# One MLP operand of two parts, squares on another engine and another split of the softmax, in a kernel of four transformer layers

## The chip, the cores and the metric
One NeuronCore of a Trainium2 chip runs the whole program. The time is what the device takes for one execution, in microseconds (us); the kernel's number is the median of several executions.

## What is computed
Two blocks of two layers each, for one sequence of 256 tokens with 1024 features, all in 32-bit floating point. Every layer adds a mixer and, in the first block, an MLP to the residual x:

```python
def sq_relu_mlp(h, w_in, w_out):          # 1024 -> 4096 -> 1024
    a = jax.nn.relu(h @ w_in)
    return (a * a) @ w_out
...
p = jax.nn.softmax(logits, axis=-1)       # in MLA, MoBA and FoX, 8 heads each
...
def l2_norm(x):                           # of GDN's q and k, per head and token
    return x * lax.rsqrt(jnp.sum(x * x, axis=-1, keepdims=True) + EPS)
```

The order is MLA attention, MLP 0, MoBA attention, MLP 1 (first block), then GDN (a gated delta rule, with a causal convolution ahead and triangular inverses by head and chunk) and FoX (attention with forget gates; second block).

## The kernel before
All weights, 140 MB, are streamed from HBM once, as 136 chunks of at most 128 x 2048 numbers (1 MB). MLA has chunks 0 to 13, MLP 0 has 14 to 45, MoBA 46 to 61, MLP 1 62 to 93, GDN 94 to 114, FoX 115 to 135. Each passes through the same five steps, each on one engine, in rings of three buffers:

- SyncE loads the chunk into `raw` (`load(c)`), once `lo(c-3)` has read that buffer.
- ScalarE rounds it to the format TensorE multiplies at full rate, fp32r: `whi` (`hi(c)`), once TensorE has finished chunk c-3.
- VectorE (POOL for six chunks of GDN) makes the rest, `wlo = raw - whi` (`lo(c)`).
- TensorE multiplies. The activations too are split, into `xh` and `xl`. A product is three matmuls into the same PSUM region: whi·xh, whi·xl, wlo·xh.

Every engine's program is one written-out list of steps, so what is queued on an engine is served in that order. TensorE's list counts chunks in quarters: `to(18, 2)` means "run chunk quarters up to quarter 2 of chunk 18", and the small steps (`score`, `turn_p`, `sums`, `bias_mm`, ...) stand between. `half(c)` and `full(c)` are the semaphore values after the second and fourth quarter of chunk c.

An MLP goes by 8 groups g of 512 hidden features. The order of its chunks is: up 0 (two chunks), up 1, down 0, up 2, down 1, and so on to down 7. In an up-projection chunk (kind `pw`) quarter m is the 128 hidden features of one weight column tile, k runs over four tiles of the 1024 inputs, and the tokens (256 columns) are what moves; two m share one PSUM bank, and groups alternate between banks 4, 5 and 6, 7. Then, by half group `hf` (512 numbers per partition): ScalarE's `relu_square` takes Relu out of PSUM and squares it; VectorE's `hidden` rounds that to `oth` and puts the rest into `otl`, which are the stationary operands of the down-projection (kind `back`, 512 columns moving).

In a softmax, `logits` (VectorE) adds mask or bias, takes the maximum and negates it; `exp` (ScalarE) also gives the sum; `divide` (VectorE) inverts the sum and multiplies the two parts of 128 and 256 columns; `turn_p` (TensorE) transposes. In GDN, `k_square` (VectorE) and `q_square` (POOL) square one head of 256 columns each, into four buffers `sqp`, and TensorE's `sums(h)` adds over the features with 8 or 16 matmuls of one column. Banks 4 to 7 of PSUM also serve all small steps in turn (`ring`), and `take` makes TensorE wait until the bank's last reader is done.

```python
mm(o, wh[:, k, s], h_[:, kk, :], kk == 0 and m % 2 == 0)
mm(o, wh[:, k, s], l_[:, kk, :], False)
tok = mm(o, wl[:, k, s], h_[:, kk, :], False)
```

These are an up-projection's three matmuls. In the profile all matmuls have line 480, all transposes 488, ScalarE's work 1354, VectorE's products and sums of two tensors 2208, those with a scalar 2211 and 2214.

Of the kernel before, what the change touches and what calls it, by code (L numbers as in the profile page):

```python
# [130 lines left out]
def bass_two_blocks(nc, A, out):  # L131

    ctx = ExitStack()
    with ctx:
# [19 lines left out]
        xh = sb("xh", [128, 8, T], F32R)  # L154
        xl = sb("xl", [128, 8, T], F32R)
# [44 lines left out]
        def rsq_tiles(n, own=6):  # L200
# [25 lines left out]
        s_sc, s_sx, s_mx, s_ex, s_dv, s_tn, s_pt, s_vl, s_oh, s_ol = (sem(n) for n in (  # L226
            "s_sc", "s_sx", "s_mx", "s_ex", "s_dv", "s_tn", "s_pt", "s_vl", "s_oh", "s_ol"))

        s_rel, s_sqr, s_hid = sem("s_rel"), sem("s_sqr"), sem("s_hid")
# [5 lines left out]
        (s_gx, s_ga, s_gg, s_beta, s_cm, s_cum, s_pre, s_acc, s_cv, s_sl, s_k2, s_q2, s_st, s_sst, s_lnr, s_rw, s_rwt, s_rT,  # L235
         s_rb, s_dt, s_ed, s_sel, s_kq, s_ba, s_sv, s_vt, s_v, s_zs) = (sem("g_" + n) for n in (
             "gx", "ga", "gg", "beta", "cm", "cum", "pre", "acc", "cv", "sl", "k2", "q2", "st", "sst", "lnr", "rw", "rwt", "rT",
# [223 lines left out]
        def tensor_program(eng):  # L461
# [35 lines left out]
            def quarter(c, q):  # L497
# [87 lines left out]
                elif kind == "pw":  # L585
                    half_, m = q // 2, q
                    b = d["pair"] + half_
                    if d["hk"] == 0 and q % 2 == 0:
                        if stage == "gdn":
                            take(b, s_pre, 2 * d["g"] + half_ + 1)  # L590
                        elif stage == "fox":
                            take(b, s_fz, 2 * d["g"] + half_ + 1)
                        else:
                            take(b, s_rel, 16 * int(stage[3]) + 2 * d["g"] + half_ + 1)
# [195 lines left out]
            def sums(h):  # L790
                L.wait_ge(s_k2, h + 1)
                L.wait_ge(s_q2, h + 1)
# [41 lines left out]
            def inv_ops(g):  # L834
                ops = (oth, otl) if g < 2 else (xh.rearrange("p k n -> p (k n)"), xl.rearrange("p k n -> p (k n)"))
                return [x[:, 1024 * (g % 2) + 512 * i:1024 * (g % 2) + 512 * i + 512] for x in ops for i in range(2)]
# [126 lines left out]
            to(1, 3)  # L963
# [16 lines left out]
            qp_T(0)  # L980
            score_pair(0)
            q_T(1)
            to(8, 2)
            qp_T(1)
            to(9, 2)
            turn_p("mla", 0)
            score_pair(1)
            turn_p("mla", 1)
# [6 lines left out]
            qp_T(2)  # L995
            q_T(2)
            to(11, 0)
            q_T(3)
            turn_p("mla", 2)
            turn_p("mla", 3)  # L1000
            score_pair(2)
# [3 lines left out]
            score_pair(3)  # L1005
            turn_p("mla", 4)
            to(11, 3)
            turn_p("mla", 5)
            turn_p("mla", 6)
            value("mla", 4)  # L1010
            turn_p("mla", 7)
            value("mla", 5)
            value("mla", 6)
            to(12, 0)
# [8 lines left out]
            to(22, 0)  # L1023
# [5 lines left out]
            to(30, 0)  # L1029
# [22 lines left out]
            to(52, 3)  # L1052
            turn_p("moba", 0)
            turn_p("moba", 1)
            to(53, 0)
            turn_p("moba", 2)
            to(53, 2)
# [10 lines left out]
            value("moba", 2)  # L1068
            score("moba", 4)
            score("moba", 5)  # L1070
            value("moba", 3)
            to(57, 3)
            turn_p("moba", 4)
            score("moba", 6)
# [40 lines left out]
            to(105, 3)  # L1115
# [15 lines left out]
            inv_0(0)  # L1131
            row_bc(5)
            to(109, 1)
            kq(4)
# [3 lines left out]
            inv_0(1)  # L1138
            row_bc(7)
            to(109, 3)  # L1140
            kq(6)
            kq(7)
            to(110, 0)
            inv_w(1, 1)
            v_T(0, 0)
            v_T(0, 1)
            inv_x(1, 1)
            inv_w(0, 1)
            v_T(1, 0)
            inv_x(0, 1)  # L1150
            inv_v(1, 1)
            inv_w(1, 2)
            v_T(1, 1)
# [44 lines left out]
            inv_x(3, 1)  # L1198
            inv_v(2, 1)
            sol(1, 0)  # L1200
# [3 lines left out]
            sol(3, 0)  # L1204
            inv_x(3, 2)
            sol(2, 0)
# [6 lines left out]
            sol(1, 1)  # L1213
            sol(0, 1)
            sol(3, 1)
# [3 lines left out]
            inv_w(3, 4)  # L1219
            sol(1, 3)  # L1220
            sol(0, 2)
# [28 lines left out]
            inv_y(3)  # L1250
            sol(4, 0)
            sol(5, 0)
            out_T(1)
            sol(6, 0)
            sol(4, 1)
            sol(5, 1)
            sol(7, 0)
            sol(6, 1)
            sol(4, 2)
            sol(5, 2)  # L1260
            sol(7, 1)
            sol(6, 2)
            sol(4, 3)
            sol(5, 3)
            sol(7, 2)
            sol(6, 3)
            sol(7, 3)
# [15 lines left out]
            to(117, 2)  # L1283
            across(1)
            to(120, 1)
            few_T(1)
            to(121, 2)
            c_mm()
            to(121, 3)
            c_T()  # L1290
            to(122, 0)
            c_bc(0)
            c_bc(1)
            c_bc(2)
            c_bc(3)
            to(126, 0)
            qk_T("fox", "k0", 0)
            qk_T("fox", "k0", 1)
            to(126, 1)
            qk_T("fox", "q0", 0)  # L1300
            qk_T("fox", "q0", 1)
            to(126, 2)
            score("fox", 0)
            score("fox", 1)
            c_bc(4)
            to(126, 3)
            score("fox", 2)
            score("fox", 3)
            c_bc(5)
            to(127, 1)  # L1310
            turn_p("fox", 0)
            to(128, 2)
            turn_p("fox", 1)
            to(128, 3)
            turn_p("fox", 2)
            to(130, 0)
            value("fox", 0)
            value("fox", 1)
            turn_p("fox", 3)
            to(130, 1)  # L1320
            qk_T("fox", "q1", 0)
            to(130, 2)
            qk_T("fox", "q1", 1)
            c_bc(6)
            c_bc(7)
            to(131, 0)
            qk_T("fox", "k1", 0)
# [4 lines left out]
            score("fox", 6)  # L1332
            score("fox", 7)
            to(132, 0)
            value("fox", 2)
            value("fox", 3)
            turn_p("fox", 4)
            to(132, 1)
            turn_p("fox", 5)
            to(133, 0)  # L1340
# [4 lines left out]
            to(133, 1)  # L1345
# [5 lines left out]
        def scalar_program(eng):  # L1351
# [68 lines left out]
            def exp(stage, j):  # L1420
# [8 lines left out]
                act(Q[:, 128:384], S[:, 128:384], ACT.Exp, bias=ng[:, 1:2], accum_out=su[:, 1:2]).then_inc(s_ex, 1)  # L1429

# [118 lines left out]
            def relu_square(i, g, hf):  # L1549
                v = g % 2  # L1550
                e = 16 * i + 2 * g + hf + 1
                c = C0[f"mlp{i}"] + (1 if g == 0 else 4 * g - 1)
                rel = view(2048 * v + 512 * hf, 512)
                sqr = view(2048 * v + 1024 + 512 * hf, 512)
                L.wait_ge(s_w, half(c) if hf == 0 else full(c))
                if g >= 2:
                    L.wait_ge(s_hid, e - 4)
# [20 lines left out]
            def conv_silu(i):  # L1578
                nm, g, hf = CONV[i // 2][0], int(CONV[i // 2][1]), i % 2
                L.wait_ge(s_cv, i + 1)  # L1580
                act((kS if nm == "k" else qS)[:, 4 * g + 2 * hf:4 * g + 2 * hf + 2, :], acc2[i % 4], ACT.Silu).then_inc(s_sl, 1)

# [32 lines left out]
            def inv_ops(g):  # L1615
                ops = (oth, otl) if g < 2 else (xh.rearrange("p k n -> p (k n)"), xl.rearrange("p k n -> p (k n)"))
                return [x[:, 1024 * (g % 2) + 512 * i:1024 * (g % 2) + 512 * i + 512] for x in ops for i in range(2)]
# [71 lines left out]
            hi(1)  # L1689
            hi(2)  # L1690
            squares("mla")
# [4 lines left out]
            rsq("mla_x")  # L1696
            proj_scale()
            hi(5)
            hi(6)
# [3 lines left out]
            c_hi(2)  # L1703
            rsq("mla_c")
            c_hi(3)
            c_hi(4)
            kv_copy(0, 0)
# [6 lines left out]
            rsq("mla_k0")  # L1714
            uq_copy(1, 0)
            uq_copy(1, 1)
            rsq("mla_q0")
# [3 lines left out]
            k_copy(0, 0)  # L1721
            rsq("mla_q1")
            k_copy(0, 1)
            q_copy(0)
            qp_copy(0)
            hi(10)
            kv_copy(1, 0)
            kv_copy(1, 1)
            k_squares(1)
            exp("mla", 0)  # L1730
            uq_copy(2, 0)
            rsq("mla_k1")
            q_copy(1)
            qp_copy(1)
            exp("mla", 1)
            uq_copy(2, 1)
            uq_copy(3, 0)
            q_squares(2)
            p_copy("mla", 0)
            p_copy("mla", 1)  # L1740
            o_hi("mla", 0)
            o_hi("mla", 1)
            rsq("mla_q2")
# [3 lines left out]
            hi(11)  # L1747
            exp("mla", 3)
            rsq("mla_q3")
            qp_copy(2)  # L1750
            k_copy(1, 0)
            k_copy(1, 1)
            q_copy(2)
            q_copy(3)
            p_copy("mla", 2)
            p_copy("mla", 3)
            hi(12)
            qp_copy(3)
            exp("mla", 4)
            o_hi("mla", 2)  # L1760
            o_hi("mla", 3)
            hi(13)
            exp("mla", 5)
            exp("mla", 6)
            exp("mla", 7)
            p_copy("mla", 4)
            p_copy("mla", 5)
            p_copy("mla", 6)
            o_hi("mla", 4)
            o_hi("mla", 5)  # L1770
            o_hi("mla", 6)
            p_copy("mla", 7)
            hi(14)
            o_hi("mla", 7)
# [5 lines left out]
            hi(16)  # L1780
            hi(17)
            hi(18)
            hi(19)
            relu_square(0, 0, 0)
            relu_square(0, 0, 1)
            relu_square(0, 1, 0)
            hi(20)
            hi(21)
            hi(22)
            hi(23)  # L1790
            relu_square(0, 1, 1)
            relu_square(0, 2, 0)
            relu_square(0, 2, 1)
            hi(24)
            hi(25)
            hi(26)
# [1999 lines left out]
```

## Time and profile before

| | us |
|---|---|
| three runs | 933.17, 934.24, 937.74 |
| median | 934.24 |
| the profiled execution, whole | 937.91 |
| its span, first to last instruction | 936.2 |

| engine | busy us | share | instructions |
|---|---|---|---|
| TensorE (PE) | 906.1 | 97% | 5944 |
| VectorE (DVE) | 625.1 | 67% | 1035 |
| ScalarE (ACT) | 512.0 | 55% | 766 |
| GpSimd (POOL) | 110.4 | 12% | 144 |

A row of a group has the count behind an x, the busy time and the mean of one instruction, then the engine's idle time ahead of such instructions and what ended it. A row of the timeline begins with start and duration in us, and names in brackets the idle time before it and its releaser. Matmuls overlap in it, so the distance of two starts says more than a duration.

### The profile page before, as it was taken

Reading aid. Unit: us, or ns where it says so; the run is one execution under the profiler, and the core shown is the slowest. Engines: PE = TensorE matmul, PEld = TensorE weight load, DVE = VectorE, ACT = ScalarE, POOL = GpSimd, SP = SyncE. Lnnn points to the kernel's source line nnn. Section 1 sums busy time; section 2 is a strip of 40 time slices with the busy share of each in tenths; the row PEclk is TensorE's granted clock in tenths of the full one; section 3 lists DMA queues with packets and bytes.
Section 4 is the critical chain, followed back from the end, with each engine's and each line's share of the span. In section 5 each row is a group of like instructions: output and inputs, shape, how many; then the busy total and the mean of one; then the engine's idle time right before and its main releaser. Section 6 shows DMA issues by size and latency. Waiting matters only on the chain.

```text
span 936.2 us, 14470 instructions
## 1 busy us (share of the span) xinstructions
PE 906.1 (97%) x5944; PEld 815.6 (87%) x5944; DVE 625.1 (67%) x1035; ACT 512.0 (55%) x766; POOL 110.4 (12%) x144
## 2 busy tenths in 40 slices
PE   5898999999999999999999999999999999999997
PEld 5776899999998888899999998999998987798886
DVE  5798766566455686655454445898886776856884
ACT  5787454345354667544454453664446664747662
POOL 0055000000000000000000000007476612000000
PEclk9999999999999999999999999999899999999999
DMA  7442356275554633455645544562511302345431
GB/s 245 146 139 87 134 182 245 90 263 178 176 192 137 224 123 141 156 183 176 211 154 207 186 174 138 182 224 90 170 56 68 136 1 90 127 164 207 134 113 46
DMA packets 61681, 142.74 MB, mean 152 GB/s; under 512 B 5296, under 2 KB 7344, under 8 KB 61616
## 3 DMA queue, kind: packets, MB, share of 16 engines
q1 hardware_dynamic: 61616, 141.82, 44.4%
q8 instruction: 47, 0.77, 0.3%
q14 instruction: 18, 0.15, 0.0%
HBM read 140.76 MB, written 1.05 MB: 151 GB/s over the span
## 4 chain that ended last, share of the span: by engine, by line
PE 84%; POOL 4%; issue 4%; DVE 4%; ACT 2%; SPq 1%; DMA 0%; POOLq 0%; DVEq 0%; ACTq 0%
PE ps L480 81%; PE ps L488 4%; POOL arena L3379 3%; DVE wlo L2208 1%; POOL wlo L3379 1%; SPq L3513 1%; POOL arena L3429 1%; ACT arena L1354 1%; ACT whi L1354 0%; DVE arena L2208 0%; DMA pint<-rel_bias_table_dram 0%; DVE oth L2208 0%; DVE X L2208 0%; ACT otl L1354 0%; DVE arena L2211 0%
## 5 line engine op out<-in xcount | busy, mean ns | idle before, releaser
L2208 DVE TENSOR_TENSOR wlo<-raw,whi 128x2048 fp32r<-128x2048 f32 (+3 forms) x130 | 287.4, 2218 | 162.1 <-ACT whi L1354 162.0
L1354 ACT ACTIVATE whi<-raw 128x2048 fp32r<-128x2048 f32 (+3 forms) x136 | 251.1, 1853 | 264.1 <-PE ps L480 225.5
L480 PE MATMUL ps<-xh,whi 128*128 128x256 f32 (+2 forms) x784 | 224.3, 286 | 0.3 <-DVE wlo L2208 0.3
L480 PE MATMUL ps<-xl,whi 128*128 128x256 f32 (+2 forms) x784 | 222.7, 284 | 0.0
L480 PE MATMUL ps<-xh,wlo 128*128 128x256 f32 (+2 forms) x784 | 222.7, 284 | 0.0
L480 PE MATMUL ps<-whi,oth 128*128 128x512 f32 x384 | 151.7, 395 | 0.0
L480 PEld LDWEIGHTS ps<-xh,whi 128*128 128x128 f32 (+2 forms) x784 | 149.9, 191 | 1.6 <-DVE wlo L2208 0.4
L480 PEld LDWEIGHTS ps<-xl,whi 128*128 128x128 f32 (+2 forms) x784 | 149.9, 191 | 1.0
L480 PEld LDWEIGHTS ps<-xh,wlo 128*128 128x128 f32 (+2 forms) x784 | 149.8, 191 | 0.4
L480 PE MATMUL ps<-whi,otl 128*128 128x512 f32 x384 | 149.7, 390 | 0.0
L480 PE MATMUL ps<-wlo,oth 128*128 128x512 f32 x384 | 149.7, 390 | 0.0
L480 PE MATMUL ps<-whi,xh 128*128 128x512 f32 (+2 forms) x264 | 104.1, 394 | 1.9 <-DVE wlo L2208 0.7
L480 PE MATMUL ps<-whi,xl 128*128 128x512 f32 (+2 forms) x264 | 100.3, 380 | 0.0
L480 PE MATMUL ps<-wlo,xh 128*128 128x512 f32 (+2 forms) x264 | 100.2, 380 | 0.0
L3379 POOL TENSOR_TENSOR arena<-arena 128x64 f32<-128x64 f32 (+1 forms) x56 | 28.2, 529 | 544.3 <-ACT arena L1354 539.4
L480 PEld LDWEIGHTS ps<-whi,otl 128*128 128x128 f32 x384 | 72.1, 188 | 15.3
L480 PEld LDWEIGHTS ps<-whi,oth 128*128 128x128 f32 x384 | 72.2, 188 | 14.1 <-issue 0.2
L480 PEld LDWEIGHTS ps<-wlo,oth 128*128 128x128 f32 x384 | 72.2, 188 | 13.9
L1354 ACT ACTIVATE arena<-ps 128x512 f32<-128x512 f32 (+3 forms) x104 | 49.5, 492 | 38.2 <-PE ps L480 28.1
L480 PE MATMUL ps<-arena 128*128 128x128 f32 (+3 forms) x384 | 63.4, 319 | 0.6 <-issue 0.5
L1354 ACT ACTIVATE arena<-arena 128x512 f32<-128x512 f32 (+5 forms) x94 | 58.4, 641 | 10.2 <-DVE arena L2211 6.0
L480 PEld LDWEIGHTS ps<-whi,xh 128*128 128x128 f32 x264 | 50.3, 191 | 11.0 <-DVE wlo L2208 2.4
(147 smaller groups left out, 1108.2 us busy)
## 6 DMA issues: line engine op xcount, KB each, us to landing
raw<-mlp_w_in_dram SPq DMA_DIRECT2D x32, 1024.0 KB, 5.2
raw<-mlp_w_out_dram SPq DMA_DIRECT2D x32, 1024.0 KB, 4.9
raw<-gdn_w_in_dram SPq DMA_DIRECT2D x16, 1024.0 KB, 5.3
raw<-moba_w_qkv_dram SPq DMA_DIRECT2D x12, 1024.0 KB, 5.1
raw<-kv_w_dram SPq DMA_DIRECT2D x8, 1024.0 KB, 5.3
raw<-fox_w_in_dram SPq DMA_DIRECT2D x8, 1024.0 KB, 5.4
raw<-mla_w_o_dram SPq DMA_DIRECT2D x4, 1024.0 KB, 5.1
raw<-moba_w_o_dram SPq DMA_DIRECT2D x4, 1024.0 KB, 6.1
```

The lines of the kernel that those rows point to most:

```text
L480: return eng.matmul(o, l, r, start=start, stop=True, skip_group_check=True)
L488: return eng.transpose(o, i, ident)
L1354: return eng.activation(o, i, f, **kw)
L2208: return eng.tensor_tensor(o, a, b, f)
L3379: return eng.tensor_tensor(o, a, b, f)
L3429: ins = eng.affine_select(out=x, in_=x, pattern=[[1, 128]], compare_op=ALU.is_ge, fill=0.0, base=-strict, channel_multiplier=-1)
L3513: eng.dma_start(o, i).then_inc(s_in, 16)
```

## The change
- **MLPs.** `xh` and `xl` become the two halves of one tensor `xhl`, [128, 8, 2, 256]. In the up-projection the first two matmuls become one with 512 moving columns, over both halves; wlo·xh stays, with 256. Each m now fills a bank (4 + m), columns 0 to 255 and 256 to 511 being the two terms. ScalarE's `half_copy` copies the right halves to SBUF, VectorE's `hidden_sum` adds the left ones and forms max(a, 0)·a, ScalarE's `hidden_hi` rounds that to `oth`, and VectorE's `hidden` only makes `otl`. The banks are free again after the adds. All groups use the same four banks.
- **GDN.** One Square on ScalarE per head (`qk_square`, q and k together, 512 columns) takes the place of `k_square` and `q_square`.
- **Softmaxes.** The maxima are written out negated by the reduction; `over_sum` (VectorE) inverts the sum, `divide` (ScalarE) multiplies by it as a scaled copy.
- **Orders.** All engines' lists are rearranged: many small steps stand some quarters earlier or later, neighbouring loads are swapped, and `levels_in` (448 KB for GDN's masks), which waits until MLA's down-projection is done, moves from behind `load(22)` to between `load(17)` and `load(16)`.

```diff
-        xh = sb("xh", [128, 8, T], F32R)
-        xl = sb("xl", [128, 8, T], F32R)
+        xhl = sb("xhl", [128, 8, 2, T], F32R)
+        xh, xl = xhl[:, :, 0, :], xhl[:, :, 1, :]
+        xpair = xhl[:, :, :, :].rearrange("p k z n -> p k (z n)")
...
-                    b = d["pair"] + half_
+                    mlp_ = stage[:3] == "mlp"
+                    b = 4 + m if mlp_ else d["pair"] + half_
+                    if d["hk"] == 0 and mlp_:
+                        take(b, s_sqr, 2 * (16 * int(stage[3]) + 2 * d["g"] + half_) + 1)
...
+                        if mlp_:
+                            mm(P[b][:, :], wh[:, k, s], xpair[:, kk, :], kk == 0)
+                            tok = mm(P[b][:, 0:256], wl[:, k, s], xh[:, kk, :], False)
+                            continue
...
             def sums(h):
                 L.wait_ge(s_k2, h + 1)
-                L.wait_ge(s_q2, h + 1)
...
-            to(103, 0)
+            to(105, 1)
             sums(0)
-            to(103, 2)
             sums(1)
-            to(104, 0)
+            to(105, 2)
             sums(2)
             sums(3)
-            to(105, 0)
+            to(105, 3)
             sums(4)
             sums(5)
-            to(105, 1)
             cum_mm()
             sums(6)
             sums(7)
-            to(105, 3)
+            to(106, 1)
             rw_T()
...
-                act(rel, P[4 + 2 * v + hf][:, :], ACT.Relu).then_inc(s_rel, 1)
-                L.wait_ge(s_rel, e)
-                act(sqr, rel, ACT.Square).then_inc(s_sqr, 1)
+                for j in range(2):
+                    ins = act(rel[:, 256 * j:256 * j + 256], P[4 + 2 * hf + j][:, 256:512], ACT.Copy)
+                ins.then_inc(s_rel, 1)
+
+            def hidden_hi(i, g, hf):
...
+                act(oth[:, o:o + 512], sqr, ACT.Copy).then_inc(s_hh, 1)
...
+            def divide(stage, j):
...
+                L.wait_ge(s_rcp, a.base + j + 1)
+                act(Q[:, 0:128], Q[:, 0:128], ACT.Copy, scale=rc[:, 0:1])
+                act(Q[:, 128:384], Q[:, 128:384], ACT.Copy, scale=rc[:, 1:2]).then_inc(s_dv, 1)
...
+            def qk_square(h):
...
+                act(view(18944 + 512 * (h % 2), 512, "p (a n) -> p a n", a=2),
+                    view(0, 4096, "p (a h n) -> p a h n", a=2, h=8)[:, :, h, :], ACT.Square).then_inc(s_k2, 1)
...
-                eng.reduce_max(mx[:, 0:1], S[:, 0:128], AX)
-                L.step(eng.reduce_max(mx[:, 1:2], S[:, 128:384], AX))
-                L.settle()
-                ts(ng, mx, -1.0, None, ALU.mult).then_inc(s_mx, 1)
+                eng.reduce_max(ng[:, 0:1], S[:, 0:128], AX, negate=True)
+                eng.reduce_max(ng[:, 1:2], S[:, 128:384], AX, negate=True).then_inc(s_mx, 1)
...
+            def hidden_sum(i, g, hf):
...
+                L.wait_ge(s_rel, e)
+                if g >= 2:
+                    L.wait_ge(s_hid, e - 4)
+                for j in range(2):
+                    s = rel[:, 256 * j:256 * j + 256]
+                    ins = tt(s, P[4 + 2 * hf + j][:, 0:256], s, ALU.add)
+                ins.then_inc(s_sqr, 1)
+                L.wait_ge(s_sqr, 2 * e - 1)
+                stt(sqr, rel, 0.0, rel, ALU.max, ALU.mult).then_inc(s_sqr, 1)
```

## Rows read from the trace of the kernel before

**Rows 1.** The page's busy times: us, share of the span, instructions.
```profile
PE 906.1 (97%) x5944; PEld 815.6 (87%) x5944; DVE 625.1 (67%) x1035; ACT 512.0 (55%) x766; POOL 110.4 (12%) x144
```
**Rows 2.** Busy us (x instructions) by stretch, then granted clock, DMA share, GB/s.
```profile
60.00:100.00 40.00, 36.71 (x222) 30.09 (x221) 34.02 (x91) 31.44 (x79) 15.79 (x38) 1.00 0.32 108
408.00:585.00 177.00, 177.00 (x1144) 162.24 (x1143) 92.66 (x74) 81.20 (x72) 0.00 (x0) 1.00 0.52 179
640.00:663.00 23.00, 22.86 (x181) 22.80 (x182) 21.35 (x48) 11.34 (x14) 15.30 (x12) 0.92 0.45 155
661.00:663.00 2.00, 2.00 (x11) 2.00 (x11) 1.69 (x11) 1.03 (x3) 0.00 (x0) 0.50 1.05 410
700.00:780.00 80.00, 76.78 (x596) 71.40 (x595) 54.80 (x105) 52.73 (x101) 38.28 (x38) 1.00 0.17 60
```
**Rows 3.** The chain that ended last, its piece in MLP 1: start, us, what.
```profile
408.18 176.79 PE ps L480 x1140
```
**Rows 4.** TensorE's timeline in MLP 1, where the kind of chunk changes.
```profile
431.19 0.40 PE L480 MATMUL ps<-whi,oth 128*128 128x512 f32 x1
...
442.09 0.28 PE L480 MATMUL ps<-xh,whi 128*128 128x256 f32 x1
...
453.61 0.40 PE L480 MATMUL ps<-whi,oth 128*128 128x512 f32 x1
```
**Rows 5.** VectorE's groups by shape, 112 to 300 us (MLP 0).
```profile
L2208 DVE TENSOR_TENSOR otl<-arena,oth 128x512 fp32r<-128x512 f32 x16 | 11.1, 692 | 0.5
...
L2217 DVE CAST oth<-arena 128x512 fp32r<-128x512 f32 x16 | 6.8, 422 | 3.5 <-ACT arena L1354 3.5
...
L2208 DVE TENSOR_TENSOR arena<-ps,cst 128x256 f32<-128x256 f32 x4 | 1.7, 420 | 1.0 <-PE ps L480 1.0
```
**Rows 6.** ScalarE's groups by shape, 112 to 300 us: Square, then Relu.
```profile
L1354 ACT ACTIVATE arena<-arena 128x512 f32<-128x512 f32 x16 | 10.1, 634 | 0.5
L1354 ACT ACTIVATE arena<-ps 128x512 f32<-128x512 f32 x16 | 9.3, 582 | 1.8 <-PE ps L480 1.8
```
**Rows 7.** Timeline in MLP 1: VectorE's difference for chunk 84, TensorE's first matmul of it.
```profile
523.11 2.29 DVE L2208 TENSOR_TENSOR wlo<-raw,whi 128x2048 fp32r<-128x2048 f32 x1 [2.41 <-ACT whi L1354]
...
531.80 0.28 PE L480 MATMUL ps<-xh,whi 128*128 128x256 f32 x1
```
**Rows 8.** Timeline at MLP 0's start: the cast of chunk 16.
```profile
117.94 1.92 ACT L1354 ACTIVATE whi<-raw 128x2048 fp32r<-128x2048 f32 x1 [2.49 <-DMA raw<-mlp_w_in_dram]
```
**Rows 9.** Groups by shape, 60 to 100 us: VectorE's divisions, ScalarE's exponentials.
```profile
L2211 DVE TENSOR_SCALAR arena<-arena,st 128x256 f32<-128x256 f32 x8 | 2.9, 357 | 0.0
L2211 DVE TENSOR_SCALAR arena<-arena,st 128x128 f32<-128x128 f32 x8 | 2.5, 307 | 0.3
...
L1354 ACT ACTIVATE arena<-arena,st 128x256 f32<-128x256 f32 x8 | 4.0, 500 | 0.0
...
L1354 ACT ACTIVATE arena<-arena,st 128x128 f32<-128x128 f32 x8 | 3.2, 397 | 1.1 <-DVE st L2211 1.1
```
**Rows 10.** Timeline in MLA: POOL's rotary work of the last query pair, TensorE's transpose.
```profile
80.22 1.12 POOL L3379 TENSOR_TENSOR arena<-arena,st 128x256 f32<-128x256 f32 x1 [0.71 <-DVE st L2214]
...
87.39 0.44 PE L488 MATMUL ps<-cst,arena 128*128 128x128 f32 x2 [2.32 <-POOL arena L3379]
```
**Rows 11.** Groups by shape, 630 to 663 us: squares and first taps on VectorE and POOL.
```profile
L2208 DVE TENSOR_TENSOR arena<-arena 128x256 f32<-128x256 f32 x7 | 7.1, 1023 | 0.1
...
L3379 POOL TENSOR_TENSOR arena<-arena 128x256 f32<-128x256 f32 x6 | 7.6, 1275 | 3.7 <-PE ps L480 3.7
```
**Rows 12.** TensorE's timeline in GDN: the last clump of small matmuls and after.
```profile
654.22 1.84 PE L480 MATMUL ps<-cst,arena 128*128 128x1 f32 x16
...
657.44 0.73 PE L480 MATMUL ps<-st,cst 128*128 128x8 f32 x6
658.31 2.43 PE L480 MATMUL ps<-cst,arena 128*128 128x1 f32 x16
...
661.17 0.41 PE L480 MATMUL ps<-xh,wlo 128*128 128x256 f32 x1
661.38 0.41 PE L480 MATMUL ps<-xh,whi 128*128 128x256 f32 x1
```

More of the change, by code:

```diff
@@ L1689, in scalar_program @@
             hi(1)
+            squares("mla")
             hi(2)
-            squares("mla")
             hi(3)
@@ L1797, in scalar_program @@
             hi(27)
+            half_copy(0, 3, 0)
+            half_copy(0, 3, 1)
+            hidden_hi(0, 3, 0)
+            squares("mlp0")
             hi(28)
-            relu_square(0, 3, 0)
-            relu_square(0, 3, 1)
             hi(29)
@@ L1931, in scalar_program @@
             hi(84)
-            relu_square(1, 5, 0)
-            relu_square(1, 5, 1)
+            half_copy(1, 5, 0)
+            half_copy(1, 5, 1)
+            hidden_hi(1, 5, 0)
             hi(85)
@@ L2907, in vector_program @@
             lo(15)
+            bias_ind(3)
             lo(16)
+            hidden_sum(0, 0, 0)
+            hidden_sum(0, 0, 1)
             lo(17)
             lo(18)
-            bias_ind(3)
             hidden(0, 0, 0)
+            hidden_sum(0, 1, 0)
+            lo(19)
+            bias_ind(4)
             hidden(0, 0, 1)
-            lo(19)
+            hidden(0, 1, 0)
+            bias_add(3)
+            hidden_sum(0, 1, 1)
+            bias_ind(5)
             lo(20)
-            bias_add(3)
@@ L2931, in vector_program @@
             bias_ind(6)
             bias_ind(7)
-            lo(26)
+            hidden(0, 2, 1)
+            hidden_sum(0, 3, 0)
             bias_add(6)
+            hidden(0, 3, 0)
             lo(27)
+            lo(28)
+            bias_add(7)
             bias_ind(8)
-            bias_ind(9)
-            bias_add(7)
-            hidden(0, 3, 0)
-            lo(28)
+            hidden_sum(0, 3, 1)
             lo(29)
             lo(30)
+            bias_ind(9)
             lo(31)
+            hidden_sum(0, 4, 0)
@@ L2957, in vector_program @@
+            lo(35)
+            lo(36)
+            bias_add(10)
+            bias_add(11)
+            hidden_sum(0, 5, 1)
+            lo(37)
+            lo(38)
             hidden(0, 5, 0)
-            bias_add(10)
-            lo(36)
-            lo(37)
-            bias_add(11)
+            lo(39)
             hidden(0, 5, 1)
-            lo(38)
-            lo(39)
+            hidden_sum(0, 6, 0)
+            hidden_sum(0, 6, 1)
             lo(40)
@@ L2967, in vector_program @@
             lo(42)
+            hidden(0, 6, 0)
+            variance(0)
             lo(43)
-            hidden(0, 6, 0)
+            hidden_sum(0, 7, 0)
+            hidden_sum(0, 7, 1)
             hidden(0, 6, 1)
@@ L3044, in vector_program @@
             lo(65)
+            hidden_sum(1, 0, 0)
+            hidden_sum(1, 0, 1)
             lo(66)
+            lo(67)
             hidden(1, 0, 0)
             hidden(1, 0, 1)
-            lo(67)
-            hidden(1, 1, 0)
-            hidden(1, 1, 1)
+            hidden_sum(1, 1, 0)
+            hidden_sum(1, 1, 1)
             lo(68)
             lo(69)
+            hidden(1, 1, 0)
             lo(70)
+            hidden(1, 1, 1)
+            hidden_sum(1, 2, 0)
+            hidden_sum(1, 2, 1)
             lo(71)
@@ L3056, in vector_program @@
             lo(73)
-            lo(74)
-            lo(75)
             hidden(1, 2, 0)
             hidden(1, 2, 1)
-            hidden(1, 3, 0)
+            lo(74)
+            hidden_sum(1, 3, 0)
+            hidden_sum(1, 3, 1)
+            lo(75)
             lo(76)
@@ L3577, in sync_program @@
             load(10)
-            load(12)
             load(11)
             load(13)
+            load(12)
+            load(15)
             load(14)
-            load(15)
             load(17)
+            levels_in()
             load(16)
@@ L3631, in sync_program @@
             load(63)
+            load(65)
             load(64)
-            load(65)
             load(66)
@@ L3662, in sync_program @@
             load(93)
+            load(96)
             load(95)
-            load(96)
             load(97)
```

757 lines of the change are left out of this document (404 added, 353 removed).

## The prediction

> **What bounds the kernel now.** I read the busy shares first: TensorE 906.1 us, 97% of the span, VectorE 67%, ScalarE 55% [rows 1]. A mean over stages says little, so next the busy time by stage: in the MLPs TensorE has no hole at all (177.00 of 177.00 us in the second), between 60 and 100 us (MLA) it is busy 36.7 of 40 and between 700 and 780 us (GDN's triangular inverses) 76.8 of 80 [rows 2]. The chain that ended last says the same by what released what: in the second MLP 176.79 us of it are unbroken TensorE [rows 3]. So in an MLP a change is worth what it takes from TensorE's own stream; outside, what it takes from a wait that TensorE really has.
>
> A busy TensorE can still be fed better or worse, and durations mislead here: one matmul lasts 0.28 or 0.39 us but they overlap. What counts is the distance between starts. From 431.19 to 442.09 us stand 48 matmuls of 512 columns: 10.90/48 = 0.2271 us each. From 442.09 to 453.61 us stand 96 of 256 columns: 11.52/96 = 0.1200 us [rows 4]. The difference, 0.1071 us for 256 columns, is the rate of the 2.4 GHz level (the granted clock is 1.00 there [rows 2]); what is left, 0.013 us, is paid once per matmul whatever its width.
>
> **MLP up-projection.** Before, a weight tile costs three 256-column matmuls (hi·xh, hi·xl, lo·xh); after, one of 512 (hi·[xh|xl]) and one of 256 (lo·xh). The columns are the same 768, one matmul is gone: 3 x 0.1200 = 0.3600 becomes 0.2271 + 0.1200 = 0.3471, 0.0129 us less. The weight of 1024 x 4096 has 8 x 32 = 256 tiles of 128 x 128, both MLPs 512: **−6.6 us**, all on the path. Bounds: zero if the mixed sequence doesn't keep the pitch of the pure ones; on the other side the 768 columns alone, 3 x 0.1071 = 0.3213 us a tile, −19.8 us, which no row comes near. I take 6.6, since both pitches are read in the very stage.
>
> The Trainium skill (TensorE: Matmul & The Clock Gate, "Back-to-back issue gap") speaks against it: by it a matmul costs its columns and some 2.5 ns. By that rule 512 fewer save 1.3 us. The rows show 13 ns.
>
> The two halves must now be added. Per half group (32 in both MLPs) ScalarE's Relu and Square of 512 (0.58 + 0.64 us) become two copies of 256 out of PSUM and one cast of 512; VectorE's cast and difference (0.42 + 0.69 us) become two adds of 256 (0.42 each by its 256-wide work), a max-times of 512 and the difference (0.69 each): about 2.2 instead of 1.1 us [rows 5, 6]. A group of 22 us then asks VectorE for four weight differences of 2.29 and 4.4 = 13.6 us, ScalarE for about 10. That lies beside TensorE and costs nothing as long as the weight differences come early: the one ending at 525.40 us is of the chunk that TensorE begins at 531.80 (one chunk stands between), 6.4 us ahead [rows 7]. This cover is the thing to lose: VectorE serves in order, and what is queued behind a `hidden_sum` that waits for ScalarE's copy is the next `lo`, on which both TensorE and, through the ring of three, SyncE's next load wait.
>
> Banks: a group now fills four banks instead of two, so the next group waits for its adds. Only groups 0 and 1 of each MLP are adjacent; elsewhere 10.9 us of down-projection lie between. There the first half has two quarters (2 x 4 tiles x 0.347 = 2.8 us) for two copies and two adds (about 1.7 us): nothing, but with 1 us to spare. In the first MLP this meets a moved step on SyncE: `levels_in`, which waits for the end of MLA's down-projection, now stands ahead of `load(16)`. Its 448 KB take 2.6 us at the stage's 179 GB/s, and the cast of chunk 16 already waited 2.49 us for its DMA and began at 117.94 us [rows 2, 8]. Copy and add of group 0 stand behind that cast and its difference. I put +0.5 us on it (0 to +3). The other swaps of loads next to each other I cost at nothing: with three ring slots both are asked for within a chunk's time.
>
> **Softmaxes (24 heads).** VectorE loses a small negation and two multiplications (0.31 + 0.36), ScalarE gains two scaled copies: by its exponentials of the same shapes 0.40 and 0.50 us, less the 0.1 us by which neighbours overlap, 0.8 us a head. Only the busy share says whether it matters: MLA from 60 to 100 us has VectorE at 34.0 and ScalarE at 31.4 of 40 [rows 2, 9]. Moving 8 x 0.8 us shifts which is fuller but frees the side that feeds the rotary terms: TensorE's one long hole, 2.32 us before 87.39, ends with POOL's rotary work, and POOL had itself waited for VectorE, until 80.22 us [rows 10]. With `over_sum` short and `rsq_b` of the queries ahead, POOL starts about 1 us sooner. I take −1.2 us for MLA (−3 to +2.5, the latter if ScalarE, the fuller engine then, is late with the copies that TensorE's transposes wait for). In MoBA and FoX TensorE is covered by projections: 0 (−1 to +1).
>
> **GDN.** 16 products of 256 columns leave VectorE and POOL (7.1 us for 7 and 7.6 for 6 in 630 to 663 us, so over 1 us each, while the two engines run side by side) and become 8 of 512 on ScalarE, 0.64 us each as its Squares in the MLP: 5.1 us, in a stretch where it is busy 11.3 of 23 [rows 2, 6, 11]. None of this is on the chain: TensorE is busy 22.86 of 23 us there. It changes when `sums` can stand: they move from quarters (103,0)…(105,1) to (105,1)…(105,3), the last four close together on two alternating buffers, each pair waiting for ScalarE behind the one before: +0.3 to +1 us, against −1 for VectorE and POOL being free ahead of the decays. Net −0.5 (−3 to +3). The inverses themselves aren't touched.
>
> **The clock.** The profiled execution lost time at 659 us: behind 16 and, 1.4 us on, 6 + 16 matmuls of 1 or 8 columns the granted clock fell to 0.50, the 1.2 GHz level, and 256 columns went at 0.213 us instead of 0.120 [rows 2, 12]. The two quarters behind it are 24 of these, 2.2 us more, and some small ones before; I put 2.8 us on it. After the change 22 such small matmuls stand in one clump, with two of 8 ahead, so I expect the same odds of a fall. The profiled run took 937.91 us, the timed ones 933.17, 934.24 and 937.74: a median that does without the fall fits (937.9 − 2.8 = 935.1).
>
> **The sum.** −6.6 + 0.5 − 1.2 − 0.5 = −7.8. On the profiled execution's 937.9 us this is 930.1; on the median of the runs, 3.7 below that execution, it is 926.4.
>
> **Rivals.**
> (A) *The per-matmul cost isn't there to save.* The 0.013 us could come with the change of weights and width rather than with each matmul, and the mixed sequence keep 0.360 us a tile. Then the MLPs give nothing and 934.2 + 0.5 − 1.2 − 0.5 = 933.0 is left. For it: only pure sequences can be read. Against: every matmul of the pure ones changes its weights too. 6%. The page of the Trainium skill named above points this way; by its 2.5 ns the time would be 1.3 us lower, 931.7, as an estimate.
> (B) *The drain holds the weights back: slower than before.* Place: VectorE's queue in the MLPs, `lo` behind `hidden_sum` and `hidden`, these behind ScalarE's `half_copy`. From half(c) the chain runs 0.8 + 0.8 + 0.7, again for the second half 2.8 us later, then 0.6 + 0.7, then `lo` 2.3: about 8.8 us, against 8.3 until TensorE needs the chunk after next. If the order lets a whole drain stand ahead of `lo`, and handing over costs a little more than I count, 1 us is lost in each of 16 groups: 926.4 + 16 = 942. It decides from the point where VectorE's lead of 6.4 us is used up; most groups have a `lo` between the halves, which speaks against. 6%.
> (C) *Given back outside*: ScalarE late in MLA, the clump of `sums` waits, the entry to the first MLP costs 2 to 3 us: −6.6 + 2.5 + 1 + 1 = −2.1, so 932. 10%.
> (D) *More than forecast*: MLA's hole closes and GDN gains 3: 934.2 − 6.6 − 2.5 − 3 = 922. 8%.
> The forecast itself, 926.4 with 923 to 929.5: 70%.
>
> **Numbers.** Faster by over 0.5% (below 929.6; 0.5% is about what a measurement of this kernel can tell): the forecast, D, and a little of C: 0.80. Same (929.6 to 938.9): most of C, A: 0.14. Slower: 0.06. The range 921 to 932 takes in D, the bounds of MLA, GDN and the clock, and C; it leaves out B.
>
> **What would show it.** Starts 0.227 and 0.120 us apart by turns in the MLPs, pairs of up-projection chunks 11.10 instead of 11.52 us long; TensorE without a hole in them; each MLP 3.3 us shorter; ScalarE's squares of 512 near 650 us. It would be wrong if the 512-column matmul or its follower took longer, or if the weight differences ended less than 1 us ahead of their chunk.

## The result, and the profile after

| | before | after |
|---|---|---|
| median of 7 runs each, us | 937.11 (933.17 to 937.74) | 931.19 (929.36 to 931.48) |
| the profiled execution, us | 937.91 | 929.36 |
| its span, us | 936.2 | 927.6 |

The ratio is 0.9943 (0.9928 to 0.9959): 0.57% faster, −5.9 us, where the forecast was −7.8 us from a base of 934.24. The time of 931.19 us lies in the range given (921 to 932), 4.8 us above the predicted 926.4.

Busy times on the page of after (us, share of the span, instructions), against [rows 1]: TensorE has 512 instructions less and is busy 6.4 us less, VectorE 5.2 us and ScalarE 19.8 us more, GpSimd 11.0 us less.

```profile
PE 899.7 (97%) x5432; PEld 785.9 (85%) x5432; DVE 630.3 (68%) x1019; ACT 531.8 (57%) x854; POOL 99.4 (11%) x136
```

The same stretches by the windows view of after (columns as in [rows 2], the MLP window starting at its own 404):

```profile
60.00:100.00 40.00, 37.05 (x216) 30.71 (x215) 29.33 (x66) 32.82 (x90) 13.93 (x33) 1.00 0.33 118
...
404.00:581.00 177.00, 177.00 (x898) 149.88 (x897) 108.79 (x107) 82.14 (x91) 0.00 (x0) 1.00 0.52 179
```

In MLP 1 TensorE still has no hole (177.00 of 177.00), though VectorE went from 92.66 to 108.79 us. The chain of waits of after has both MLPs as one unbroken piece of TensorE (start, us, what):

```profile
111.40 181.17 PE ps L483 x1100
...
403.67 175.26 PE ps L483 x884
```

The second answers to [rows 3]: 176.79 became 175.26, that is −1.5 us with 256 matmuls less, where −3.3 was forecast. TensorE's timeline of after shows why. First the places where the kind of chunk changes, as in [rows 4], then a stretch inside an up-projection:

```profile
437.20 0.39 PE L483 MATMUL ps<-xhl,whi 128*128 128x512 f32 x1
...
448.49 0.40 PE L483 MATMUL ps<-whi,oth 128*128 128x512 f32 x1
...
459.44 0.39 PE L483 MATMUL ps<-xhl,whi 128*128 128x512 f32 x1
```
```profile
440.01 0.40 PE L483 MATMUL ps<-xhl,whi 128*128 128x512 f32 x1
440.25 0.28 PE L483 MATMUL ps<-xhl,wlo 128*128 128x256 f32 x1
440.37 0.40 PE L483 MATMUL ps<-xhl,whi 128*128 128x512 f32 x1
440.61 0.28 PE L483 MATMUL ps<-xhl,wlo 128*128 128x256 f32 x1
440.72 0.40 PE L483 MATMUL ps<-xhl,whi 128*128 128x512 f32 x1
```

Two up-projection chunks (32 weight tiles) took 448.49 − 437.20 = 11.29 us, so 0.3528 us a tile: neither the 0.3600 of before nor the forecast 0.3471. A 512-column matmul is followed after 0.23 to 0.24 us, a 256-column one after 0.11 to 0.12. The down-projection behind it took 10.95 us against 10.90 before [rows 4]. One cycle of up and down is 22.24 us against 22.42: 0.18 us saved, 16 times is 2.9 us. The two pieces of the chain together, 182.69 + 176.79 before and 181.17 + 175.26 after, give 3.0.

The cover held. VectorE's and ScalarE's groups by shape, 112 to 300 us in after, against [rows 5, 6]:

```profile
L2300 DVE TENSOR_TENSOR arena<-ps,arena 128x256 f32<-128x256 f32 x32 | 12.0, 418 | 11.9 <-ACT arena L1360 11.9
L2306 DVE SCALAR_TENSOR_TENSOR arena<-arena 128x512 f32<-128x512 f32 x16 | 11.1, 693 | 0.5
...
L2300 DVE TENSOR_TENSOR otl<-arena,oth 128x512 fp32r<-128x512 f32 x16 | 10.6, 685 | 0.1
```
```profile
L1360 ACT ACTIVATE arena<-ps 128x256 f32<-128x256 f32 x32 | 10.5, 381 | 23.4 <-PE ps L483 23.4
L1360 ACT ACTIVATE oth<-arena 128x512 fp32r<-128x512 f32 x16 | 9.9, 627 | 4.8 <-DVE arena L2306 4.8
```

Two adds of 0.418, 0.693 and 0.685 make 2.2 us a half group, as forecast.

### The profile page after: what moved, and what is told of

It reads as the page before. It is cut to its first block, busy times and chain, and to the rows that moved or that the text cites. A ratio compares the mean times of both kernels' runs of the same rounds, so it can differ in the third digit from the quotient of the medians.

```text
span 927.6 us, 13495 instructions
## 1 busy us (share of the span) xinstructions
PE 899.7 (97%) x5432; PEld 785.9 (85%) x5432; DVE 630.3 (68%) x1019; ACT 531.8 (57%) x854; POOL 99.4 (11%) x136
## 4 chain that ended last, share of the span: by engine, by line
PE 86%; POOL 4%; issue 4%; DVE 3%; ACT 1%; DMA 1%; SPq 0%; POOLq 0%; DVEq 0%; ACTq 0%
PE ps L483 82%; PE ps L491 4%; POOL arena L3498 3%; POOL wlo L3498 1%; DMA X<-x_dram 1%; DVE wlo L2300 1%; POOL arena L3542 1%; ACT arena L1360 1%; ACT whi L1360 0%; DVE arena L2300 0%; DVE xhl L2300 0%; DVE oth L2300 0%; DVE X L2300 0%; ACT otl L1360 0%; DVE arena L2303 0%
## 5 line engine op out<-in xcount | busy, mean ns | idle before, releaser
L483 PE MATMUL ps<-xhl,whi 128*128 128x512 f32 (+3 forms) x1056 | 282.6, 341 | 0.0
L483 PE MATMUL ps<-xhl,wlo 128*128 128x256 f32 (+2 forms) x784 | 221.3, 282 | 0.0
L483 PEld LDWEIGHTS ps<-xhl,whi 128*128 128x128 f32 (+2 forms) x1056 | 180.0, 188 | 24.9
L483 PE MATMUL ps<-whi,xhl 128*128 128x512 f32 (+2 forms) x528 | 166.0, 385 | 1.4 <-DVE xhl L2306 0.7
L483 PEld LDWEIGHTS ps<-xhl,wlo 128*128 128x128 f32 (+2 forms) x784 | 147.8, 189 | 0.8
L483 PEld LDWEIGHTS ps<-whi,xhl 128*128 128x128 f32 x528 | 98.8, 189 | 19.2 <-DVE wlo L2300 1.6
L483 PE MATMUL ps<-wlo,xhl 128*128 128x512 f32 (+2 forms) x264 | 99.7, 378 | 0.0
L1360 ACT ACTIVATE arena<-ps 128x256 f32<-128x256 f32 (+3 forms) x136 | 52.0, 419 | 76.9 <-PE ps L483 69.2
L483 PEld LDWEIGHTS ps<-arena 128*128 128x128 f32 (+1 forms) x384 | 53.7, 190 | 6.3 <-issue 1.8
L483 PEld LDWEIGHTS ps<-wlo,xhl 128*128 128x128 f32 x264 | 50.1, 190 | 7.4
```

The costliest lines, as they stand in the source:

```text
L483: return eng.matmul(o, l, r, start=start, stop=True, skip_group_check=True)
L1360: return eng.activation(o, i, f, **kw)
```

## The experiments

Ratios are to the runs of before made beside each. Those runs of before, 56 besides one of 5080 us that the comparisons leave out, fall into three clusters: 22 between 933.0 and 934.8 us, 14 between 935.5 and 936.6, 20 between 937.5 and 939.2. Their median is 936.0.

**The merge alone undone.** Everything as after, the wide matmul split in two.

```diff
-mm(P[b][:, :], wh[:, k, s], xpair[:, kk, :], kk == 0)
+mm(P[b][:, 0:256], wh[:, k, s], xh[:, kk, :], kk == 0)
+mm(P[b][:, 256:512], wh[:, k, s], xl[:, kk, :], False)
```

> The changed kernel with the merge alone undone: three matmuls of 256 columns into the same two halves of the bank, all adds, banks, lists and other edits as changed. Theory (the merge is worth what its pitch shows): up-projection pairs of chunks last 11.52 us again instead of 11.29, 16 x 0.23 = 3.7 us more than the changed kernel, about 935. Rival (the merge's matmuls are worth the forecast 6.6 and something else in the MLPs takes 3 us): 6.6 more, about 938. Rival (the MLP gain is hidden by the drain): less than 1.5 more.

Measured: 935.32 us, ratio 0.9986 (0.9972 to 1.0000). Its chain has the second MLP so:

```profile
407.47 176.75 PE ps L483 x1140
```

That is before's 176.79 again [rows 3], and the first MLP's piece, 182.77 us, is before's 182.69. So the 512 matmuls are the whole gain of the MLPs: 1.5 us in this one. By the ratios the merge is worth 0.9986 − 0.9943 = 0.43%, 4.0 us (the intervals leave some 2 us either way), by the trace 3.0.

**The merge alone done.** MLPs and the first block's orders as after, the softmaxes and GDN's squares with their places as before.

> The changed kernel with its MLPs as they are, but the softmaxes and GDN's squares and their order as in the kernel before: what is left is the merged operand and the orders of the first block. The trace gave the merge 3.7 us (32 pairs of matmuls in 11.29 us instead of 11.52 by chunk pair). Theory (the merge is what makes the change faster, all the rest about 1 us): 932 to 933, that is 3.7 to 4.5 under the kernel before (936 to 937), ratio 0.9955 to 0.996. Rival 1 (the moved softmax and GDN steps are worth the forecast 1.7 us or more, hidden by the clock's scatter so far): 934 or over. Rival 2 (they cost something that the merge pays for): 930 or under.

Measured: 931.72 us, ratio 0.9966 (0.9950 to 0.9982). The merge, with the first block's orders, gives 0.34%, 3.2 us, so the larger part; the rest of the change 0.14 to 0.23% by these two experiments, 1.3 to 2.2 us, with intervals as wide as that. In this trace the MLPs' pieces are 180.75 and 174.82 us, 3.9 us less than before together, where after's are 3.0 less. The reason stands under the next experiment.

**Are the changes of width what eats the saving?** The same matmuls in another order. By quarter, four wide ones and then four narrow ones:

```diff
     mm(P[b][:, :], wh[:, k, s], xpair[:, kk, :], kk == 0)
-    tok = mm(P[b][:, 0:256], wl[:, k, s], xh[:, kk, :], False)
...
+for k in range(4):
+    tok = mm(P[b][:, 0:256], wl[:, k, s], xh[:, 4 * d["hk"] + k, :], False)
```

> The changed kernel with the up-projection's matmuls of a quarter in another order: first the four of 512 columns, then the four of 256, so 2 changes of width a quarter in place of 8. The trace of the changed kernel shows 0.3528 us a tile where the pure pitches add up to 0.3471. Theory W (a change of width costs some 6 ns a pair): 3 of 4 pairs lose that cost, a quarter takes 1.393 us instead of 1.411, over 128 quarters 2.2 us less than the changed kernel. Rival L (the 512-column matmul over the joined operand is itself slower, by layout or by its neighbours on the other engines): the tile keeps 0.353 us and the time that of the changed kernel.

And by two quarters, eight wide ones and then eight narrow ones, on the same pattern:

> The changed kernel with blocks of eight: in each half chunk eight matmuls of 512, then eight of 256. Alternating, a pair took 0.3528 us; in blocks of four 0.3500; the pure pitches add up to 0.3471. In blocks of four the first four of 512 of a chunk went at 0.227, later ones behind narrow ones at 0.228 to 0.236. Theory W (the cost sits at the changes of width and the matmuls just behind them): the later wide ones of a block are back at 0.227 and a pair takes about 0.3485, 1 us less than in blocks of four. Rival (every wide matmul of this stage is slower once narrow ones have run): 0.350 again.

Measured: by quarter 930.62 us, ratio 0.9943 (0.9924 to 0.9962); by two quarters 928.62 us, ratio 0.9924 (0.9901 to 0.9947). The ratios overlap with after's; the trace is sharper. TensorE's timeline by two quarters (rows of equal matmuls put together):

```profile
437.83 1.98 PE L483 MATMUL ps<-xhl,whi 128*128 128x512 f32 x8
439.64 1.12 PE L483 MATMUL ps<-xhl,wlo 128*128 128x256 f32 x8
...
448.98 0.40 PE L483 MATMUL ps<-whi,oth 128*128 128x512 f32 x1
...
459.88 0.84 PE L483 MATMUL ps<-xhl,whi 128*128 128x512 f32 x3
```

Eight wide ones start over 439.64 − 437.83 = 1.81 us, 0.226 each: the pure pitch. The two chunks took 11.15 us, 0.3484 a tile, and the down-projection 10.90 again: a cycle of 22.05 us. With a change of width at every matmul it was 22.24, at every fourth 22.12 (11.20 and 10.92). The chain pieces of the second MLP, by quarter and by two quarters:

```profile
403.71 174.70 PE ps L483 x884
```
```profile
404.34 174.14 PE ps L483 x884
```

So blocks come nearer to the forecast: 176.79 − 174.14 = 2.65 us of the forecast 3.3 per MLP, where by turns it was 1.5. By quarter, 2.2 us less than after was expected; the two pieces give 1.1.

But the change of width is not by itself what costs. The traces hold stretches where the same order, by turns, ran at the forecast's pitch. In the one with the merge alone, MLP 1 has both in turn, groups 0 and 1 at its start and then group 2 behind a down-projection:

```profile
411.78 0.40 PE L483 MATMUL ps<-xhl,whi 128*128 128x512 f32 x1
...
422.87 0.40 PE L483 MATMUL ps<-xhl,whi 128*128 128x512 f32 x1
...
437.59 0.39 PE L483 MATMUL ps<-xhl,whi 128*128 128x512 f32 x1
...
448.88 0.40 PE L483 MATMUL ps<-whi,oth 128*128 128x512 f32 x1
```

The first two rows are 32 pairs apart, 422.87 − 411.78 = 11.09 us, 0.3466 a pair; so are the other two, 11.29 us, 0.3528 a pair. Six traces have this order. In them all 72 up-projections that follow a down-projection take 0.3528 to 0.3530 us a pair. Of the twelve stretches of groups 0 and 1, five run at 0.347 us past their first eight pairs, six at 0.353, and one changes from one to the other and back. So the pieces of MLP 1 are 174.82 us in three of these traces and 175.21 to 175.26 in the other three, and the merge as written is worth 3.0 to 3.9 us over both MLPs; in blocks of eight it is (182.69 − 180.15) + 2.65 = 5.2. What decides between the two paces (what stands ahead of the stretch and the weight loads are candidates) was not separated.

**Does VectorE's load matter (rival B)?** One more product of 512, into memory that nobody reads, in each half group.

```diff
+stt(view(12000, 512), rel, 0.0, rel, ALU.max, ALU.mult)
 stt(sqr, rel, 0.0, rel, ALU.max, ALU.mult).then_inc(s_sqr, 1)
```

> The changed kernel with one more VectorE operation of 0.69 us in every half group of the MLPs (the max-times, also written to an unused place), 22 us more work for VectorE. It measures the cover that I called the thing to lose. Theory (the weight differences come 6 us early in most groups): nothing but at the chunks where the lead is now under 1 us (0.3 us at chunk 71, 0.7 at 75, 1.1 at 17), so 0 to 2 us. Rival B of the forecast (VectorE is close to the bound in the MLPs): over 5 us.

Measured: 931.96 us, ratio 0.9956 (0.9935 to 0.9976). MLP 1 by the windows view, and its chain piece:

```profile
408.00:585.00 177.00, 177.00 (x899) 150.01 (x899) 118.17 (x124) 82.58 (x89) 0.00 (x0) 1.00 0.52 179
```
```profile
407.12 174.82 PE ps L483 x884
```

VectorE carries 118.17 instead of 108.79 us there and TensorE has no hole. The piece is even 0.44 us shorter than after's 175.26; groups 0 and 1 took the fast pace here.

**Softmax and GDN, each undone alone.** First `over_sum` and `divide` together on VectorE again, with the maxima negated in a step of their own; then the squares in `k_square` and `q_square` with the lists of GDN around them as before.

> The changed kernel with the softmaxes alone as before: negation and both multiplications on VectorE at the places of the list where it now only inverts the sums, nothing on ScalarE. Theory (the move is worth about 1 us in MLA and nothing under the projections of MoBA and FoX): 1 us slower than the changed kernel, the difference between 60 and 100 us. Rival (ScalarE is the one that is late): as fast or faster by up to 1 us.

> The changed kernel with GDN as before: squares on VectorE and POOL, and the lists of all engines between the stage's first small steps and its end taken from the kernel before. Theory (0.5 us or less is to be had there, since TensorE is not short of work while the squares are made): the same time within 1 us, the same falls of the clock. Rival (VectorE and POOL hold each other up, and freeing them brings the decays forward): 2 to 3 us slower.

Measured: 931.45 us, ratio 0.9956 (0.9938 to 0.9974), and 931.31 us, ratio 0.9957 (0.9938 to 0.9976). Against after's 0.9943 each is worth 0.13 to 0.14%, 1.2 to 1.3 us, which the intervals don't tell from nothing; by the times alone they are 0.3 and 0.1 us slower than after's 931.19.

**The clock.** GDN's sums as 128 equal columns instead of one, in after and in before.

```diff
-ins = mm(P[b][:, a:a + 1], sqp[...][...], K("ones")[:, 0:1], True)
+ins = mm(P[b][:, 128 * a:128 * a + 128], sqp[...][...], K("ones"), True)
```

> The changed kernel with the 32 one-column matmuls of GDN's sums made 128 columns wide (same number, same weights, columns of ones; only the first column is read). Transposes of 128 columns start 0.11 us apart like the one-column ones, so the work takes no longer. Theory K (the clump of one-column matmuls is what lets the granted clock fall, and the fall costs what the quarters behind it lose): no fall near 655 us, the time of an execution that has one drops by 1.4 to 2.8 us. Rival (the fall comes from something else, such as waits or the stage): the fall stays, 0 us.

> The kernel before with the same widening of the sums. Theory K: the fall of 6.8 us at 659 us is gone, 2.5 to 3 us faster than the kernel before, about 934.2, the level of its two fastest runs. Rival: the two levels of the kernel before have another cause, and the time stays at 937.

Measured: 929.72 us, ratio 0.9926 (0.9906 to 0.9947), and 934.90 us, ratio 0.9982 (0.9968 to 0.9996). Against after's 931.19 the median is 1.5 us lower, against the 936.47 of before's runs beside it 1.6. TensorE's timeline and windows (busy us, granted clock, DMA share, GB/s), first of after:

```profile
645.61 1.84 PE L483 MATMUL ps<-cst,arena 128*128 128x1 f32 x16
...
655.00:660.00 5.00, 5.00 (x33) 0.69 0.37 142
660.00:665.00 5.00, 5.00 (x43) 0.97 0.00 0
```

and of after with wide sums:

```profile
647.15 1.95 PE L483 MATMUL ps<-cst,arena 128*128 128x128 f32 x16
...
655.00:660.00 5.00, 5.00 (x46) 1.00 0.68 211
660.00:665.00 5.00, 5.00 (x45) 1.00 0.00 0
```

Sixteen small matmuls last 1.95 instead of 1.84 us, so the width is nearly free, and the granted clock stays at 1.00. All nine traces with one-column sums show a fall to 0.50 (1.2 GHz) that begins between 654 and 660 us and lasts 3.4 or 6.8 us; none of the four with wide sums does. Nor do the timed runs of before with wide sums have the upper cluster, but for one: 11 of 12 lie between 933.3 and 935.3 us.

The two kernels with wide sums share their falls: both have the one near 35 us, of 3.4 us, and none in GDN. That makes their traces the fair pair for a comparison by stage. The borders are the chain's pieces for the MLPs and the row of the residual addition that ends GDN. Before, with narrow and then with wide sums:

```profile
114.28 182.69 PE ps L480 x1356
...
791.08 0.76 DVE X L2214
```
```profile
114.36 182.69 PE ps L480 x1356
408.24 176.79 PE ps L480 x1140
...
788.52 0.76 DVE X L2214
```

And after, the same:

```profile
782.57 0.76 DVE X L2306
```
```profile
113.22 180.93 PE ps L483 x1100
405.25 175.21 PE ps L483 x884
...
782.61 0.76 DVE X L2306
```

| stage, us | before | after | difference | before, wide sums | after, wide sums | difference |
|---|---|---|---|---|---|---|
| start and MLA | 114.28 | 111.40 | −2.88 | 114.36 | 113.22 | −1.14 |
| MLP 0 | 182.69 | 181.17 | −1.52 | 182.69 | 180.93 | −1.76 |
| MoBA | 111.21 | 111.10 | −0.11 | 111.19 | 111.10 | −0.09 |
| MLP 1 | 176.79 | 175.26 | −1.53 | 176.79 | 175.21 | −1.58 |
| GDN | 206.11 | 203.64 | −2.47 | 203.49 | 202.15 | −1.34 |
| FoX and end | 145.08 | 145.04 | −0.04 | 145.05 | 145.02 | −0.03 |
| sum | 936.16 | 927.61 | −8.55 | 933.57 | 927.63 | −5.94 |

The pair with wide sums adds up to −5.9 us; the medians of before and after differ by 5.9, those of the two wide kernels by 5.2. The other pair differs by 2.6 us more, all of it in the two stages where the clock fell: before's trace has the fall near 35 us and one of 6.8 us in GDN, after's only one of 3.4 us in GDN.

**Both repairs together, and the other fall.** Blocks of two quarters and wide sums; then the same with eight transposes of a constant in TensorE's first hole near 30 us.

> The changed kernel with both repairs: the up-projection goes through eight wide matmuls and then eight narrow ones (11.15 instead of 11.29 us by chunk pair in the trace of that experiment, 16 groups: 2.2 us), and GDN's sums are 128 columns wide (no clock fall near 656 us, 2.8 us where there was one). Theory (both add): 927 (926 to 928). Rival (the two overlap, or the clock falls in another place once it holds at 656 us): 928.5 or more, no better than the better of the two alone (928.62).

> The kernel of the run before with eight transposes of a constant added in TensorE's hole near 30 us, ahead of the transposes of the compressed keys and values; their result is never read. They fill 1.1 of two holes of about 1.4 us. Theory (the clock fall at 35 us, 3.4 us at 1.2 GHz, follows from how little TensorE did in the 5 us ahead of it): no fall there in the profile, and 1 to 1.5 us less, 925.5 to 926.5. Rival (the second hole alone suffices for the fall, or the fall has another cause): the row at 35 us still shows 0.50 and the time is that of the kernel without the filler.

Measured: 926.23 us (925.31 to 928.56), ratio 0.9914 (0.9895 to 0.9934), and 926.75 us, ratio 0.9913 (0.9895 to 0.9931). The first is the fastest kernel here, 0.86% under before. By the ratios it is 0.3% under after, with intervals that touch (0.9928 and 0.9934); by the times 5.0 us, and its slowest run, 928.56, is below after's fastest, 929.36. The filler stands where it should, and changes nothing:

```profile
30.73 1.04 PE L491 MATMUL ps<-cst 128*128 128x128 f32 x8
32.23 1.06 PE L491 MATMUL ps<-cst,arena 128*128 128x128 f32 x8 [0.46 <-DVE arena L2309]
34.73 0.62 PE L491 MATMUL ps<-cst,arena 128*128 128x128 f32 x2 [1.44 <-DVE xhl L2312]
```

Its windows, here of TensorE alone, still show the fall behind the second hole:

```profile
36.00:38.00 2.00, 2.00 (x6) 0.50 0.96 348
```

Nine traces show this fall (in one it lasts 6.8 us), and in four (after's, the one by quarter, the softmax undone, the merge alone) it is missing though the holes are alike there. Whether filling the second hole too would end it was not tried.

## Why the prediction was right or wrong

- **The base failed: 2.9 of the miss of 4.8.** The text took 934.24, the median of three runs, and argued that "a median that does without the fall fits". Over 7 runs the median of before is 937.11, over the 56 others 936.0. With three clusters within 6 us, three values could not carry that argument, and the profiled execution at 937.9 was no outlier. The terms make up the rest, −5.9 instead of −7.8.
- **MLP merge, −6.6: right mechanism, mis-sized; of the terms the one that failed.** It measured −3.0 in after's trace, −3.0 to −3.9 over the six traces of this order, 3.2 and 4.0 by the ratios. The step that failed is "both pitches are read in the very stage": they were read in pure sequences, and the change alternates them. The text named the mixed sequence as the bound of zero and then took the full value. Behind a down-projection a pair takes 0.3528 us instead of the 0.3471 added up; in blocks of eight 0.3484, and the MLPs gain 5.2. Rival A's extreme (0.360 a tile) didn't come, half of its way did. Yet the 13 ns per matmul are there to save in this very order: where it takes the fast pace, a pair needs 0.3466 us. Saved per matmul left out, that is 6.0 ns in after, 10.1 in blocks. The Trainium skill (TensorE: Matmul & The Clock Gate, "Back-to-back issue gap") has 2.5 ns per matmul, as an estimate 1.3 us for 512; every one of these rows is above it.
- **Cover by VectorE and ScalarE: right, but by half a microsecond.** TensorE shows no hole in either MLP, even with 22 us more on VectorE, so rival B falls. The text's sign of being wrong, a weight difference that ends less than 1 us ahead of its chunk, did come: in after the difference of chunk 71 (the first of the two in the row) ends at 453.48 us, 0.5 us ahead of TensorE's first matmul of that chunk, where before's ended 6.6 us ahead; at chunk 75 it is 0.9 (the expectation above had read 0.3 and 0.7). With the extra product it is 0.3 us at both.

```profile
451.19 4.50 DVE L2300 TENSOR_TENSOR wlo<-raw,whi 128x2048 fp32r<-128x2048 f32 x2 [0.32 <-ACT whi L1360]
...
454.00 0.39 PE L483 MATMUL ps<-whi,oth 128*128 128x512 f32 x1
```

- **Entry to MLP 0, +0.5: nothing.** The chain piece from 111.40 us is unbroken for 181.17 us; the cast and the load of chunk 16 didn't hold anything.
- **MLA, −1.2: the size about right, the reason wrong.** The hole of 2.32 us [rows 10] shrank to 1.45. But with the softmax undone it is 1.39 us, in the same place, so the division on ScalarE isn't what brings POOL's rotary work sooner; the order of the small steps is what remains, and which of them does it was not separated. The row of after, then that of the softmax undone:

```profile
84.21 0.44 PE L491 MATMUL ps<-cst,arena 128*128 128x128 f32 x2 [1.45 <-POOL arena L3498]
```
```profile
84.25 0.44 PE L491 MATMUL ps<-cst,arena 128*128 128x128 f32 x2 [1.39 <-POOL arena L3502]
```

  Another wait for POOL grew in its place, 1.37 us ahead of 62.18 us where before has 0.77 and 0.33. All of TensorE's waits for POOL in MLA add up to 3.75 us before and 3.16 after, and to 3.1 to 3.2 in every trace of the changed orders. As a whole, from TensorE's first projection matmul to the first MLP, the two traces of before's orders took 101.2 and 101.3 us, the four of after's with the same single fall near 35 us 100.2 to 100.7: 0.5 to 1.1 us gained. Four without the fall took 98.2 to 99.7.
- **GDN, −0.5: more than forecast.** With wide sums on both sides it took 1.3 us less, with narrow ones 2.5. So in these two traces the fall in GDN cost before 2.6 us (the text had 2.8) and after 1.5. "The same odds of a fall" was right, nine of nine; of the eight traces of changed kernels with narrow sums, four have a fall of 3.4 us and four one of 6.8. With the squares undone, and a fall as short as after's, GDN took 204.46 us against 203.64: some 0.8 us of the gain are theirs with their lists, by one trace.
- **MoBA and FoX, 0: right.** MoBA changed by 0.1 us. From the end of GDN to the end of the program it is 145.0 to 145.1 us in all thirteen traces, with or without the softmax's new split.
- **The sum.** With the falls alike it is −1.1 for the start and MLA, −3.3 for the MLPs, −0.1 for MoBA and −1.3 for GDN. That −7.8 came as near to −5.9 as it did is partly luck: the merge gave about half of its term, GDN more than its own, and the entry's +0.5 didn't come.
- **The rest of the forecast.** Rival C's time (932) came nearly true with none of its mechanisms. The chance of 0.80 for faster by over 0.5% held by the ratio, narrowly: 0.57%, with an interval that reaches to 0.41%. By the text's own bound in us (below 929.6) it did not, since that hung on the base.

## What to carry to other kernels

A pitch read in a pure sequence need not hold for an alternation: look for the order that will be issued, in more than one stretch, since here one order had two paces; and group equal widths where banks allow it. Freedom from holes says nothing of how little was left: read the lead of what feeds the bottleneck, too. A base for the forecast needs as many runs as the clusters of the kernel ask for; three values 4.6 us apart are no median. Compare stages between traces whose clock falls are alike, and end every stage at the same step of the program. Where a product has one column only because its result has one, widening it to fill time can be free and keep the clock up.

## What the runs showed of the hardware beyond the forecast

- 512 and 256 columns by turns have two paces, 0.3528 and 0.3466 us a pair, the slow one in all 72 up-projections behind a down-projection; in blocks of eight a pair takes 0.3484, where the pure pitches add up to 0.3471; and the pure 512-column stretch behind the alternation takes 10.95 instead of 10.90 us.
- Matmuls of one column count as busy in the profile (1.84 us for 16), and the granted clock fell behind them in nine traces of nine; at 128 columns, for 0.11 us more, in none of four.
- TensorE's holes near 31 and 34 us were followed by a fall in nine traces of thirteen, and shortening the first from 1.34 to 0.46 us didn't prevent it in the one trace that tried.
